# The boundary between mixer and feed-forward layer, taken in pieces: a fused two-block layer stack on one core

## What is computed

```
for layer in range(DEPTH):
    u = rms_norm(x, norm_gains[layer, 0])
    mix = ab_mixer(...) if layer % 2 == 0 else hgrn2_mixer(...)
    x = x + rms_norm(mix, norm_gains[layer, 1])
    u = rms_norm(x, norm_gains[layer, 2])
    ff = conv_ffn(u, ffn_w_up[layer], ffn_conv_w[layer], ffn_conv_b[layer], ffn_w_down[layer])
    x = x + rms_norm(ff, norm_gains[layer, 3])

def rms_norm(x, gain):
    y = xf * lax.rsqrt(jnp.mean(jnp.square(xf), -1, keepdims=True) + EPS)
    return (y * gain.astype(jnp.float32)).astype(x.dtype)
```

## Time and profile before

| | us |
|---|---|
| median of 3 runs | 1110.27 |
| lowest, highest | 1109.67, 1110.66 |
| the profiled execution | 1109.99 |
| its span, first to last instruction | 1108.7 |
| PE busy | 1009.6 (91%) |
| DVE busy | 748.4 (68%) |
| ACT busy | 629.1 (57%) |
| mean granted clock of PE | 0.964 of full |

### The profile page before, as it was taken

How to read it: one execution, slowest core, us unless ns; L and a number is a source line. 1 busy time by engine, 2 the same in 40 slices (tenths; PEclk the granted TensorE clock), 3 DMA queues, 4 the chain that set the end, 5 groups by cost and what they waited for, 6 DMA issues and landing times. The chain is left out here.

```text
span 1108.7 us, 16064 instructions
## 1 busy us (share of the span) xinstructions
PE 1009.6 (91%) x6436; PEld 863.1 (78%) x6436; DVE 748.4 (68%) x1129; ACT 629.1 (57%) x997; POOL 71.0 (6%) x51
## 2 busy tenths in 40 slices
PE   7999889998979799999589999997999969999996
PEld 5777768976757798887478888877878858888885
DVE  4775556555454666756667777776797567777776
ACT  5564746344545654445575566565644676656654
POOL 0000000000000014210000000000443000000000
PEclk9999989999989889999889999998999989999999
DMA  7633433652223333222336565553433545556550
GB/s 292 228 114 115 125 122 115 190 170 67 68 68 122 120 109 96 95 76 93 117 118 196 184 194 185 188 169 128 152 126 121 165 149 166 182 185 191 188 189 38
DMA packets 43563, 158.55 MB, mean 143 GB/s; under 512 B 4960, under 2 KB 5344, under 8 KB 43360
## 3 DMA queue, kind: packets, MB, share of 16 engines
q1 hardware_dynamic: 42480, 154.23, 43.4%
q0 software_dynamic: 576, 2.10, 0.6%
q10 hardware_dynamic: 432, 1.20, 0.3%
HBM read 156.45 MB, written 1.05 MB: 142 GB/s over the span
## 5 line engine op out<-in xcount | busy, mean ns | idle before, releaser
L376 DVE TENSOR_TENSOR w_lo<-raw,w_hi 128x1024 fp32r<-128x1024 f32 x288 | 366.9, 1277 | 200.4 <-ACT w_hi L367 200.2
L367 ACT ACTIVATE w_hi<-raw 128x1024 fp32r<-128x1024 f32 x288 | 302.7, 1055 | 226.4 <-PE psum L390 226.0
L390 PE MATMUL psum<-u_both,w_hi 128*128 128x512 f32 x704 | 250.8, 399 | 0.3 <-DVE u_both L584 0.2
L390 PE MATMUL psum<-u_both,w_lo 128*128 128x256 f32 x704 | 197.7, 281 | 0.0
L390 PE MATMUL psum<-w_hi,u_hi 128*128 128x512 f32 x432 | 178.5, 413 | 12.8 <-DVE u_lo L584 7.8
L390 PE MATMUL psum<-w_lo,u_hi 128*128 128x512 f32 x432 | 172.1, 398 | 0.0
L390 PE MATMUL psum<-w_hi,u_lo 128*128 128x512 f32 x432 | 171.8, 398 | 0.0
L390 PEld LDWEIGHTS psum<-u_both,w_hi 128*128 128x128 f32 x704 | 132.5, 188 | 33.5 <-DVE u_both L584 1.1
L390 PEld LDWEIGHTS psum<-u_both,w_lo 128*128 128x128 f32 x704 | 133.1, 189 | 1.5
L390 PE MATMUL psum<-u_hi,w_hi 128*128 128x256 f32 x384 | 114.5, 298 | 1.4 <-DVE w_lo L376 1.4
L390 PE MATMUL psum<-u_lo,w_hi 128*128 128x256 f32 x384 | 111.9, 291 | 0.0
(11 more groups left out here) (284 smaller groups left out, 1244.1 us busy)
## 6 DMA issues: line engine op xcount, KB each, us to landing
raw<-in_pieces SPq DMA_DIRECT2D x288, 512.0 KB, 3.5
feat<-in_norm_gains POOLq DMA_DIRECT2D x4, 512.0 KB, 4.0
const<-in_table SPq DMA_DIRECT2D x1, 1464.0 KB, 8.7
x_res<-in_x SPq DMA_DIRECT2D x1, 512.0 KB, 5.0
x_res<-in_x ACTq DMA_DIRECT2D x1, 512.0 KB, 5.2
out_x<-x_res SPq DMA_DIRECT2D x1, 512.0 KB, 2.7
out_x<-x_res ACTq DMA_DIRECT2D x1, 512.0 KB, 2.8
cols<-in_cols SPq DMA_DIRECT2D x1, 380.0 KB, 4.1
```

The source lines that it names most:

```text
L367: act.q.activation(w_hi[i % SPLIT][:, :], raw[i % RAW][:, :], ACT.Copy).then_inc(act.done, act.mark("hi", i))
L376: dve.q.tensor_tensor(w_lo[i % SPLIT][:, :], raw[i % RAW][:, :], w_hi[i % SPLIT][:, :].bitcast(F32), ALU.subtract).then_inc(dve.done, dve. ...
L390: return pe.q.matmul(o, lhs, rhs, start=start, stop=stop, **kw)
```

## The change

It is made at both boundaries (`"ab"` after the first mixer, `"c"` after the second). Both token tiles of half c = 0 are now squared by ACT and multiplied by the gain by DVE straight out of PSUM, between the two last weight pieces that the mixer's loop splits; DVE and ACT take turns on a bank. The mean of the first half's squares, plus eps, is written as a bias (`mix_part`). After the loop half c = 1 follows, tile by tile: square, Ln with that bias, Exp, and `x_res` of the tile. x is squared per tile; instead of the scaled copy DVE writes a diagonal matrix of 1/rms per tile, and PE multiplies `x_res` blocks with it, all eight of tile 0 and then all eight of tile 1, as ordinary matmuls in float32 and no longer as transposes. The copies to `mix`, the two table loads and `normed` of this norm are gone; silu's table set is loaded before the features. `pe_up` waits per pair of k, and takes its products in that order.

```diff
@@ act_ab, dve_ab @@
-        for _ in range(3):
-            act_hi()
+        act_hi()
+        act_hi()
+        act_mix_first(0, "yab")
+        act_hi()
         act_mix_end(0, "ab")
...
@@ the boundary @@
+    def act_mix_square(l, c, t):
+        act.wait_ge(pe, f"half{t}", f"mix{l}", c)
+        act.q.activation(normed[:, t, c * NC:(c + 1) * NC], psum[:, 2 * c + t, :], ACT.Square,
+                         accum_out=mix_sums[:, c, t:t + 1]).then_inc(act.done, act.mark("mix_sq", l, c, t))
+
+    def dve_mix_gain(l, c, t):
+        cs = slice(c * NC, (c + 1) * NC)
+        dve.wait_ge(pe, f"half{t}", f"mix{l}", c)
+        dve.q.tensor_tensor(mix_gained[:, t, cs], psum[:, 2 * c + t, :], post_gain[:, cs], ALU.mult).then_inc(
+            dve.done, dve.mark("mix_gain", l, c, t))
+
+    def act_mix_first(l, y):
+        act.wait_ge(pe, "turned", y, 3)
+        act_mix_square(l, 0, 0)
+        act.wait_ge(dve, "mix_gain", l, 0, 1)
+        act_mix_square(l, 0, 1)
+        act.wait_ge(act, "mix_sq", l, 0, 1)
+        act.q.activation(mix_part, mix_sums[:, 0, :], ACT.Identity, scale=1.0 / D, bias=eps1).then_inc(
+            act.done, act.mark("mix_part", l))
+
+    def dve_mix_first(l):
+        dve.q.wait_ge(in_post_gain, 16 * (2 * l + 1))
+        dve_mix_gain(l, 0, 1)
+        dve.wait_ge(act, "mix_sq", l, 0, 0)
+        dve_mix_gain(l, 0, 0)
 
     def act_mix_end(l, name):
-        for c in range(2):
-            act_token_half(f"mix{l}", c, mix[:, :, c * NC:(c + 1) * NC], c)
-        act_add_normed(name, mix, evicted(f"mix{l}", 0) + evicted(f"mix{l}", 1))
+        rstd = post_rstd[name]
+        act.wait_ge(act, "mix_part", l)
+        for t in range(ST):
+            act_mix_square(l, 1, t)
+            act.wait_ge(act, "mix_sq", l, 1, t)
+            act.q.activation(rstd[:, t:t + 1], mix_sums[:, 1, t:t + 1], ACT.Ln, scale=1.0 / D,
+                             bias=mix_part[:, t:t + 1]).then_inc(act.done, act.mark("ln", name, t))
+            act.wait_ge(act, "ln", name, t)
+            act.q.activation(rstd[:, t:t + 1], rstd[:, t:t + 1], ACT.Exp, scale=-0.5).then_inc(
+                act.done, act.mark("rstd", name, t))
+        norm = f"n{l}2"
+        for t in range(ST):
+            act.wait_ge(dve, name, "x", t)
+            act.q.activation(normed[:, t, :], x_res[:, t, :], ACT.Square, accum_out=norm_sums[norm][t]).then_inc(
+                act.done, act.mark("square", norm, t))
+            act.wait_ge(act, "square", norm, t)
+            act_rstd(norm_sums[norm][t], D, norm_rstd[norm][t], norm, t)
 
     def dve_mix_end(l, name):
...
+        for t in range(ST):
+            dve.wait_ge(act, "mix_sq", l, 1, t)
+            dve_mix_gain(l, 1, t)
+            dve.wait_ge(act, "rstd", name, t)
+            dve.wait_ge(dve, "mix_gain", l, 1, t)
+            dve.q.scalar_tensor_tensor(x_res[:, t, :], mix_gained[:, t, :], post_rstd[name][:, t:t + 1], x_res[:, t, :],
+                                       ALU.mult, ALU.add).then_inc(dve.done, dve.mark(name, "x", t))
+        for t in range(ST):
+            dve.wait_ge(act, "rstd", f"n{l}2", t)
+            dve.q.tensor_scalar(rms_diag[:, t, :], ident, norm_rstd[f"n{l}2"][t], None, ALU.mult).then_inc(
+                dve.done, dve.mark("diag", f"n{l}2", t))
+
+    def pe_scaled_features(name, free):
+
+        for t in range(ST):
+            pe.wait_ge(dve, "diag", name, t)
+            for kk in range(KT // 2):
+                for step in free(kk):
+                    pe.wait_ge(*step)
+                for j in range(2):
+                    k = 2 * kk + j
+                    last = mm(psum[:, 4 + kk, (j * ST + t) * P:(j * ST + t + 1) * P], x_res[:, t, k * P:(k + 1) * P],
+                              rms_diag[:, t, :], loose=True)
+                if t == ST - 1:
+                    last.then_inc(pe.done, pe.mark("turned", name, kk))
@@ pe_up @@
-            pe.wait_ge(dve, f"n{l}2", "lo", 2 * part + 1)
...
-            for i in range(2):
-                for kk in range(KT // 2):
-                    k, bank = part * KT // 2 + kk, 2 * (j % 2) + i
...
+            for pair in range(2):
+                pe.wait_ge(dve, f"n{l}2", "lo", 2 * part + pair)
+                for i in range(2):
+                    for kk in (2 * pair, 2 * pair + 1):
+                        k, bank = part * KT // 2 + kk, 2 * (j % 2) + i
...
@@ pe_ffn, act_ffn, dve_ffn @@
-        pe_norm(f"n{l}2", free)
+        pe_scaled_features(f"n{l}2", free)
...
-    def act_ffn(l, x):
-        act_norm(f"n{l}2", [(u_f, gain_of(f"n{l}2"))], (x, "x"))
+    def act_ffn(l):
+        act.q.preload_act_table_set("silu_and_others")
+        act_features(f"n{l}2", [(u_f, gain_of(f"n{l}2"))])
...
-        dve_norm(f"n{l}2", [(u_f, gain_of(f"n{l}2"))])
+        dve_features(f"n{l}2", [(u_f, gain_of(f"n{l}2"))])
@@ act_c (and dve_c with dve_mix_first(1)) @@
+            elif n == 6:
+                act_mix_first(1, "yc")
         act_mix_end(1, "c")
```

More of the change, by code:

```diff
@@ L653, in pool_post_gain @@
         pool.q.dma_start(post_gain, gain).then_inc(in_post_gain, 16)
[L655 to L680, removed]
     qk_gain, lam_in = (view(par, PAR[name][0], n, DA_DIM) for name, n in (("qk_gain", 2), ("lam_in", 4)))
@@ L2473, in dve_ab @@
         dve_yab(3)
-        for _ in range(3):
-            dve_lo()
+        dve_lo()
+        dve_lo()
+        dve_mix_first(0)
+        dve_lo()
         dve_mix_end(0, "ab")
@@ L2501, in pool_ab @@
         pool_post_gain(0, 1, (dve, "yab", "lo", 3))
-    mix = view(scr, 0, ST, D)
     mix_gained = view(scr, 4096, ST, D)
-    def pe_mix_out(l, u, free):
-        for c in range(2):
-            pe_chunk(f"mix{l}", c, "tokens", y_t, u, c, free)
-    def act_mix_end(l, name):
-        for c in range(2):
-            act_token_half(f"mix{l}", c, mix[:, :, c * NC:(c + 1) * NC], c)
-        act_add_normed(name, mix, evicted(f"mix{l}", 0) + evicted(f"mix{l}", 1))
-    def dve_mix_end(l, name):
-        for c in range(2):
-            dve_token_half(f"mix{l}", c, mix[:, :, c * NC:(c + 1) * NC], c)
-        dve_add_normed(name, mix, evicted(f"mix{l}", 0) + evicted(f"mix{l}", 1), 2 * l + 1, mix_gained)
@@ L2522, in act_mix_out @@
[L2522 to L2533, removed]
-        dve_add_normed(name, mix, evicted(f"mix{l}", 0) + evicted(f"mix{l}", 1), 2 * l + 1, mix_gained)
+    mix_sums, mix_part = tiny(2, ST), tiny(ST)
@@ L2551, in pe_up @@
             hi, lo = (view(w[s], 0, 2, KT // 2, P) for w in (w_hi, w_lo))
-            pe.wait_ge(dve, f"n{l}2", "lo", 2 * part + 1)
             if j >= 2:
                 pe.wait_ge(dve, "up_sum", l, j - 2)
-            else:
-                for c in range(2):
-                    for step in evicted(f"mix{l}", c):
-                        pe.wait_ge(*step)
-            for i in range(2):
-                for kk in range(KT // 2):
-                    k, bank = part * KT // 2 + kk, 2 * (j % 2) + i
-                    mm(psum[:, bank, :], hi[:, i, kk, :], u_both[:, k, :, :].rearrange("p a s -> p (a s)"), k == 0,
-                       False, True)
-                    last = mm(psum[:, bank, 0:S], lo[:, i, kk, :], u_f[0][:, k, :], False, k == KT - 1, True)
+            for pair in range(2):
[3 more added lines that the diff above has]
+                        k, bank = part * KT // 2 + kk, 2 * (j % 2) + i
+                        mm(psum[:, bank, :], hi[:, i, kk, :], u_both[:, k, :, :].rearrange("p a s -> p (a s)"), k == 0,
+                           False, True)
+                        last = mm(psum[:, bank, 0:S], lo[:, i, kk, :], u_f[0][:, k, :], False, k == KT - 1, True)
             last.then_inc(pe.done, pe.mark("used", n))
@@ L3169, in dve_c @@
                 dve_feature("yc", 3, YC)
+            elif n == 6:
+                dve_mix_first(1)
         dve_mix_end(1, "c")
@@ L3199, in act_program @@
         act_ab()
-        act_ffn(0, "ab")
+        act_ffn(0)
         act_c()
-        act_ffn(1, "c")
+        act_ffn(1)
         act.wait_ge(dve, "f1", "x", 1)
```

## The result

| us | before | changed |
|---|---|---|
| median | 1110.23 (6 runs) | 1104.67 (6 runs) |
| lowest, highest | 1109.67, 1110.66 | 1099.68, 1106.11 |
| profiled execution, its span | 1109.99, 1108.7 | 1106.11, 1104.8 |

The ratio is 0.9945 with an interval of 0.9932 to 0.9958. The change saves 5.6 us, against 6.1 forecast (1104.2, range 1100.5 to 1107.0).

The account below looks back on a forecast made before the run. PE, 91% busy, bounds the kernel; boundary relays of ACT and DVE leave it idle. 2 x 2.0 + 0.48 + 2 x 0.83 = 6.1 us off the profiled 1109.99; against the median, 1104.2, range 1100.5 to 1107.0.

Parts of the forecast that it names:

- The relay: ACT and DVE alternating short steps between mix's last product and PE's restart: restart at 904.95 instead of 909.37, 4.4 us earlier.
- Products dearer than transposes: PE's products by the diagonal before the features: each costs two transposes, 0.44 us at half clock.
- the later of the two cases: At the boundary, full clock returns 4.7 us after PE's restart, after the first result; the layer starts 1.8 us earlier.
- Cheap products: Rival, chance 0.07: a product by the diagonal costs no more than a transpose; 9.6 us gained, 1100.6.
- bare weight loads: Rival, chance 0.05: PE doesn't load the diagonal products' weights beside the running pass; 3.3 us slower, 1113.5.
- factor of four: Rival, chance 0.02: a float32 product by the diagonal costs four transposes, 0.88 us at half clock; no change, 1110.4.
- The layer starts 2.0 sooner at each boundary: Feed-forward layer's first product after mix: 1.8 to 2.25 us earlier, taken as 2.0 at each boundary.
- 0.48 once for the clock: First boundary: the clock rises ahead of the layer's first products, which had run at half clock; 0.48 us saved.
- 0.83 twice for the table load: Inside each layer, between two strips: without silu's table load the taps start 0.83 us sooner, gained at each boundary.
- the stop of 0.93: PE's wait inside each layer for a weight piece's low part, 0.93 us; forecast to go with the table load.
- The late clock: Rival, chance 0.03: full clock returns only 4.7 us after the layer's first product; no change, 1110.5.

Follow-up runs that it names:

- w1: Changed kernel with five extra float32 matmuls of constants, result unread, on PE right behind mix's last product at each boundary: 1100.16 us.
- w3: Changed kernel with scaled copies and transposes for the diagonal products, seven extra matmuls in PE's idle time, and silu's table load behind the features: 1101.47 us.
- u1: Changed kernel with the first half's squares and gain products moved behind the last weight piece: 1106.23 us.
- q1: Changed kernel with the old wait and loop order in `pe_up`, four k of low parts instead of two: 1105.12 us.
- p1: Changed kernel with scaled copies of x by DVE and PE transposes in place of the diagonal matrices and float32 products: 1102.24 us.
- t2: Kernel before with only silu's table load moved, into ACT's idle time ahead of the first strip's copy: 1108.25 us.
- b1: Kernel before with ten extra matmuls of 128 x 512 in PE's idle time at each boundary, ahead of `pe_norm`: 1108.79 us.
- after_again: The changed kernel itself, unaltered, run again in the second series: 1104.10 us.
- t1: Kernel before with only silu's table load moved, ahead of the gained features: 1111.54 us.

## Why the prediction was right, step by step

**The relay.** Measured from the end of mix's last product at the second boundary: tile 0's diagonal after 5.0 us (forecast 5.2), PE's restart after 5.07 (5.24), tile 1's diagonal after 6.9 (6.9). Durations read from neighbouring rows (the square out of PSUM at the end of the feed-forward layer, the diagonal of other layers) held to 0.04.

**Products dearer than transposes.** Forecast 0.44 a product at half clock; measured twenty passes in 4.6 us. Features forecast 9.87 us after mix's end, measured 9.73 and 9.36. The second is shorter since full clock came back 3.7 us after PE's restart there, inside the 3.5 to 4.7 that I had from the kernel before. At the first it took 5.8, outside it. That cost nothing beyond the forecast, because a return behind the first ten products was already in it as the later of the two cases. Cheap products (1100.6) didn't happen; nor did bare weight loads (1113.5): 32 passes in 5.6 to 6.6 us are far from 9. The Trainium skill's factor of four (TensorE: Matmul & The Clock Gate, Terms) is refuted here: at full clock w1's products and w3's transposes, both sixteen and both with clock 1.0, take 3.92 (a short wait included) and 1.94. The factor is two.

**The layer starts 2.0 sooner at each boundary.** Measured 1.91 and 2.28, the second just beyond the 1.8 to 2.25 that I had. u1 shows the early half's part (1.4 to 1.6 of gap), q1 the finer wait's (0.8 to 0.9), p1 what the diagonal takes back, and w1 that half clock is why. What the other cuts in the relay are worth (some 1.1 of idle time) is a remainder and not shown by a kernel.

**0.48 once for the clock, 0.83 twice for the table load.** Together 2.14; the lead-ins gave 2.06, which is 0.43 once (18.58 less 18.15) and 0.82 twice. t2 shows the load's part by itself: of the stop of 0.93, 0.13 was left, so the load had made 0.80 of it, against 0.83 and 0.1 left in the forecast. In the changed kernel 0.1 to 0.2 was left.

**The sum.** 6.1 forecast, 6.25 in the rows of the two steps, 5.6 between medians (6.3 between those of the second series). That the rows agree is the test of the forecast; that the medians come so close is in part luck, since single executions lie up to 5 us from their median for reasons outside the change. The profiled executions differ by 3.9, and the rows for that are not at the boundary. These are stretches of the first block in the kernel before, in the changed one and in b1:

```profile
150.00:185.00 35.00, 28.69 (x152) 24.53 (x151) 18.38 (x29) 17.38 (x34) 0.00 (x0) 0.90 0.34 105
```

```profile
150.00:185.00 35.00, 28.72 (x139) 24.34 (x138) 16.92 (x27) 15.88 (x32) 0.00 (x0) 0.85 0.31 100
```

```profile
150.00:185.00 35.00, 27.35 (x169) 23.77 (x168) 20.07 (x34) 18.41 (x35) 0.00 (x0) 1.00 0.38 113
```

The code there is the same in all three. Where the clock is granted less, PE starts fewer matmuls in the same stretch (152, 139, 169), and mix's last product ends later: 546.8, 548.7, 542.0. The profile of t2 has a clock of 1.00 there too, and 544.5; those of after_again, p1, w1 and w3, with 0.85, have 547.0 to 548.0. b1's profiled execution is the one of 1103.80, 5 us under its own median. I didn't foresee this spread: executions of the changed kernel from 1099.68 to 1106.11, and of the kernel before, with more runs, from 1105.27. That it makes the low runs is read from these profiles and was not tested by a kernel of its own.

**The late clock (0.03)** didn't come to the changed kernel, but it came to t1: half clock for 4.9 us from the first product of the layer and some 2.2 us lost, where I had 4.7 and 2.35.

## What to carry to other kernels

When a serial stretch between two dense ones is shortened, cost PE's own work in it at the clock that PE will have after idling. A step with few passes behind the last dependency (four transposes) can beat one that starts earlier with more work (ten products of two passes), and idle time filled with matmuls that nobody reads took another 3.3 us off the two gaps, where the whole change had taken 4.2. In the kernel before, the same filling gave the gaps only 1.05: it pays where PE's own work is what the next step waits for. Price new instructions by the same shape elsewhere in the trace: here that was good to some per cent. A table load costs only where its engine is late, so it belongs into an idle stretch that the timeline shows, not simply early.

## What was not expected of the hardware

- Sixteen transposes at half clock were followed by full clock at the second boundary of the kernel before and at t1's first (its first strip product took 0.50), but not at t1's second, where half clock lasted some 9 us from PE's restart. Between them and the products PE idled 0.72 us there, 1.02 at the first boundary.
- Half clock began at different times after the same last product. Worked out from the mean granted clock over the idle time of 5.07 us in the changed kernel, it was 1.9 us into it at the second boundary (mean 0.69) and 4.0 us at the first (mean 0.90). Even so both restarted at half clock.
- With the clock kept over the boundary, five extra matmuls of two passes of 0.43 each took 4.45 us of PE's time and delayed nothing: the products by the diagonal started 5.07 us after mix's last product with them and without.
